# A fused two-block transformer kernel: output weights split beside the last z columns, output products tile by tile, head norms held back

## The reference

```
for layer in (0, 1):                               # first_block
    h = rms_norm(x) * (1 + scale) + shift          # shift, scale, gate = silu(c) @ ada_w + ada_b
    q, k.., v.., z = split(h @ w_in)               # 16 query heads, 4 key/value heads, 64 wide
    q, k = rope(rms_norm(q)), rope(rms_norm(k))    # the head norm
    o = attention(q, k, v)                         # layer 0: compressed + selected + window branch, gated
    x = x + gate * ((o * silu(z)) @ w_out)         # layer 1: one causal branch
# second_block ("layer 2"): the same skeleton with two kinds of heads, no z; two groups of 512 columns
# are normed before w_out; then PEER: h2 @ w_query, product keys, top 16, 16384 experts, final norm
```

## Time and profile before

| | |
|---|---|
| median of 3 runs | 1398.65 us (1395.99 to 1399.7) |
| the profiled execution | 1397.4 us, span 1396.0 us |
| PE busy | 1301.8 us (93%) |
| DVE busy | 1068.0 us (77%) |
| ACT busy | 592.2 us (42%) |
| POOL busy | 308.5 us (22%) |
| mean granted TensorE clock | 0.970 |

### The profile page before, as it was taken

One profiled execution on the slowest core, in us unless ns is written; L12 is line 12 of the kernel. 1 busy time (PEld: TensorE's weight loads), 2 busy tenths in 40 slices (PEclk: granted clock), 3 DMA queues, 4 the chain that ended last, 5 costly groups with the idle time before them and its releaser, 6 DMA issues.

```text
span 1396.0 us, 22037 instructions
## 1 busy us (share of the span) xinstructions
PE 1301.8 (93%) x8323; PEld 1125.2 (81%) x8323; DVE 1068.0 (77%) x2304; ACT 592.2 (42%) x1101; POOL 308.5 (22%) x199
## 2 busy tenths in 40 slices
PE   5898888988899789999999999999999999999997
PEld 5587754676498548999999999999988888888886
DVE  5586895688567868999958888888966666666666
ACT  0444681446232623455544444444443333333332
POOL 0364003371303032579990000000000000000000
PEclk9999899998999779999999999999999999999999
DMA  9867441666269416154444444444455555555552
GB/s 352 289 228 281 167 137 60 226 242 235 81 240 401 143 48 252 64 181 154 177 153 164 141 147 142 146 151 149 142 211 193 183 191 185 191 187 187 189 185 102
DMA packets 89935, 254.73 MB, mean 182 GB/s; under 512 B 8176, under 2 KB 15600, under 8 KB 89456
## 3 DMA queue, kind: packets, MB, share of 16 engines
q1 hardware_dynamic: 57424, 193.79, 39.9%
q10 hardware_dynamic: 32416, 59.66, 11.8%
HBM read 252.37 MB, written 1.05 MB: 182 GB/s over the span
## 4 chain that ended last, share of the span: by engine, by line
PE 66%; DVE 15%; POOL 7%; issue 4%; ACT 3%; DMA 3%; SPq 1%; ACTq 0%; POOLq 0%; DVEq 0%
PE bank L1692 25%; PE bank L1684 21%; PE bank L666 5%; PE bank L1963 4%; DVE arena L420 3%; PE bank L774 2%; POOL head_ms L797 2%; DVE u_lo L658 2%; POOL u_lo L1724 2%; PE bank L1090 2%; PE bank L992 1%; PE bank L901 1%; PE bank L692 1%; PE bank L545 1%; DVE arena L943 1%
## 5 line engine op out<-in xcount | busy, mean ns | idle before, releaser
L1684 PE MATMUL bank<-h_hi,u_hi 128*128 128x256 f32 x632 | 182.8, 289 | 4.0 <-POOL u_lo L1724 2.9
L1684 PE MATMUL bank<-h_hi,u_lo 128*128 128x256 f32 x632 | 178.7, 283 | 0.0
L1684 PE MATMUL bank<-h_lo,u_hi 128*128 128x256 f32 x632 | 178.7, 283 | 0.0
L2146 POOL TENSOR_SCALAR stat<-stat 128x1 f32<-128x1 f32 x2 | 0.4, 192 | 657.0 <-ACT arena L2143 657.0
L1684 PEld LDWEIGHTS bank<-h_hi,u_hi 128*128 128x128 f32 x632 | 121.0, 191 | 4.8 <-issue 1.8
L420 DVE CUSTOM_DVE_ANT_0 arena<-arena 128x1024 f32<-128x1024 f32 x80 | 117.3, 1480 | 7.0 <-DMA arena<-in_ada_t 6.0
L1684 PEld LDWEIGHTS bank<-h_lo,u_hi 128*128 128x128 f32 x632 | 121.1, 192 | 0.0
L1684 PEld LDWEIGHTS bank<-h_hi,u_lo 128*128 128x128 f32 x632 | 120.9, 191 | 0.0
L2059 ACT ACTIVATE u_hi<-raw 128x1024 fp32r<-128x1024 f32 x64 | 67.9, 1062 | 108.1 <-PE bank L1692 108.1
L1684 PE MATMUL bank<-h_hi,v_hi 128*128 128x256 f32 x392 | 112.9, 288 | 0.9 <-POOL v_lo L1724 0.9
L2059 ACT ACTIVATE v_hi<-raw 128x1024 fp32r<-128x1024 f32 x64 | 67.9, 1062 | 107.1 <-PE bank L1692 107.1
(11 more groups left out here) (275 smaller groups left out, 3552.2 us busy)
## 6 DMA issues: line engine op xcount, KB each, us to landing
raw<-in_u SPq DMA_DIRECT2D x128, 512.0 KB, 3.5
raw<-in_v SPq DMA_DIRECT2D x128, 512.0 KB, 4.3
arena<-in_ada_t SPq DMA_DIRECT2D x80, 512.0 KB, 4.6
arena<-in_ada_w SPq DMA_DIRECT2D x12, 512.0 KB, 12.1
raw<-in_nsa_w_in ACTq DMA_DIRECT2D x3, 2048.0 KB, 10.6
arena<-in_moba_w_in ACTq DMA_DIRECT2D x3, 2048.0 KB, 14.4
arena<-in_w_in ACTq DMA_DIRECT2D x3, 2048.0 KB, 10.0
arena<-in_w_query ACTq DMA_DIRECT2D x3, 2048.0 KB, 8.4
```

The lines of the kernel that those rows point to most:

```text
L1684: last = pe.matmul(zbank[k].t[:, 0:S], u[:, c, :], h[:, c, :], start=n == 0, stop=n == 3 * DC - 1)
```

## The change

Five things are changed. (1) The four parts of `second` are split beside the columns of `z1` (layer 2: beside `vb`), and its weights are therefore loaded beside `z0` (layer 2: beside `kb`), not at the start of attention. (2) In layers 0 and 1 the last column of `z1` is issued in step 0 of attention, in bank 7. (3) `rest` issues `second` of tile 0, then `first` of tile 1, then `second` of tile 1; tile 0's activations are split in step n-2 of attention, the subtraction on VectorE, in place of that step's `trickle(1)`. (4) `head_norm` is not issued behind `head_power` but held until the next tile's products and splits have been issued. (5) `trickle` units are shared out anew: 1 after a split tile (was 2), 3 after a z column (was 2), 6 after `qa` (was 4), 4+2+5 in `rest` (was 4+4+3); the last gate rows of layer 1 are no longer forced at the end of layer 0's `rest`. The fourth part of `kv1` is subtracted by GpSimd.

```diff
+    current, owed, row_free = [], [0], [False]
+    def next_row():
+        row_free[0] = False
+        m_row = load_silu(2, Y)
+        def next_silu():
+            make_silu(m_row)
+            fillers.remove("layer 0")
+        soon(next_silu, 6.0)
 def trickle(n):
                 if not fillers or isinstance(fillers[0], str):
+                    if "layer 0" in fillers[0:1] and row_free[0]:
+                        next_row()
...
+    held_seconds = []
+    def settle_held():
+        while held_seconds:
+            b, second = held_seconds.pop(0)
+            b.free = second()
     def settle_use(b, second, steps):
+        settle_held()
         trickle(steps)
-        b.free = second() if callable(second) else second
+        if callable(second):
+            held_seconds.append((b, second))
+        else:
+            b.free = second
... project
+                if ahead and c % 4 == 3:
+                    ahead.step()
+            settle_held()
             run_later()
-            if ahead:
-                ahead.step(2)
... project_split
                     if ahead:
                         ahead.step()
+                    if c == 3:
+                        settle_held()
-            settle_use(b, use(t, b.t[:], m), 2)
+            settle_use(b, use(t, b.t[:], m), 1)
... project_cols_split
-        for i in range(tile.n):
-            b = proj_bank()
+        def column(i, b):
             hi, lo, s = tile.parts[i]
...
             if ahead:
                 ahead.step()
+            settle_held()
             run_later()
             b.free = use(i, b.t[:, 0:S], m)
             trickle(steps)
             if i == 0:
                 load_all(loads)
+        for i in range(tile.n - (held_bank is not None)):
+            column(i, proj_bank())
+        if held_bank is not None:
+            return lambda: column(tile.n - 1, held_bank)
... attend
                 scores(p + 1)
+            if p == 0 and held:
+                held()
...
-            if p < n and (p or not causal_keys or len(branches) == 1):
+            if p == n - 2:
+                tile_halves()
+            elif p < n and (p or not causal_keys or len(branches) == 1):
                 trickle(1)
... gated_out
+        def second_tile(t, turns):       # the old loop's body: 24 products and add_rows(1, t, n, b, m)
         def rest(begin_next, turn_next, place_next, loads):
-            for t in range(NT):
-                split_h(t, G, oz_mark[t])
-            second.step(2)
+            split_h(1, G, oz_mark[1])
             trickle(4)
+            second_tile(0, None)
+            run_later()
+            begin_next()
+            trickle(2)
             first_chunks(1, range(DC))
-            second.step(2)
-            trickle(4)
+            load_all(loads)
             run_later()
-            for t in range(NT):
-                ...
-                if t == 0:
-                    begin_next()
-                    load_all(loads)
-                    trickle(3)
+            trickle(5)
+            second_tile(1, turns)
             if layer == 0:
-                ensure(1, (4, 5))
-                m_row = load_silu(2, Y)
-                ...
-                soon(next_silu, 8.0)
+                row_free[0] = True
-        return tail, rest
+        return tail, lambda: split_h(0, V, oz_mark[0]), rest
...
-    kv1 = Parts(columns(w_in, at_kv + WT), WT, False, [V] * 4)
+    kv1 = Parts(columns(w_in, at_kv + WT), WT, False, [V, V, V, G])
-        project_cols_split(z0, z_cols(zT, 0), z1, (out0,))
-        project_cols_split(z1, z_cols(zT, 1))
+        project_cols_split(z0, z_cols(zT, 0), z1, (out0, out1), 3)
+        last_column = project_cols_split(z1, z_cols(zT, 1), out1, held_bank=banks[7])
-        load_all((out1,))
...
-        project_cols_split(moba_z0, z_cols(zT, 0), moba_z1)
-        project_cols_split(moba_z1, z_cols(zT, 1))
+        project_cols_split(moba_z0, z_cols(zT, 0), moba_z1, (moba_out1,), 3)
+        last_column = project_cols_split(moba_z1, z_cols(zT, 1), moba_out1, steps=3, held_bank=banks[7])
-        load_all((moba_out1,))
...
-        project_cols_by_tile(qa, q_use(0), qb, (kb,), 4)
+        project_cols_by_tile(qa, q_use(0), qb, (kb,), 6)
-        project_cols_split(kb, kb_use, vb_tile)
+        project_cols_split(kb, kb_use, vb_tile, (mix_out1,))
-        project_split(vb_tile, v_use(vb))
+        project_split(vb_tile, v_use(vb), mix_out1)
-        load_all((mix_out1,))
```

More of the change, by code:

```diff
@@ L903, in add_outputs, with attend @@
         return inst
[L905 removed]
+    def attend(branches, q_of, bias_of, first_of, causal_keys, marks, v_marks, begin, done, tail, tile_halves, loads, sink=None, held=None):
         spare_pair[0] = 4
@@ L1101, in tail @@
             first_chunks(0, chunks)
+        def second_tile(t, turns):
+            x_hi, x_lo = (h[:, :, t * P:(t + 1) * P] for h in (h_hi, h_lo))
+            for n, cs in enumerate(halves):
+                b = proj_bank()
+                T.need(b.free, h_split[t])
+                for c in cs:
+                    if t == NT - 1 and c == DC - 3:
+                        turns()
+                    hi, lo, s = second.parts[c // 2]
+                    T.need(second.marks[c // 2])
+                    last = products(three(x_hi[:, c, :], x_lo[:, c, :], hi[:, c % 2, :], lo[:, c % 2, :]), b.t[:],
+                                    c == cs[0], c == cs[-1])
+                    if t == NT - 1 and c % 2 == 1:
+                        split_read[s] = m = T.did(last)
+                if t < NT - 1:
+                    m = T.did(last)
+                h_read[0] = m
+                add_rows(1, t, n, b, m)
+            pe_us[0] += 5.5
@@ L1481, in branch @@
                     lambda h, k: vs[i][:, k, (h // GQA) * HD:(h // GQA + 1) * HD], lambda h: h // GQA, gates[:, i + 1])
-        tail, rest = gated_out(out0, out1, 0, [b[1] for b in bufs])
+        tail, tile_halves, rest = gated_out(out0, out1, 0, [b[1] for b in bufs])
         attend([branch(0), branch(1)], lambda h, t: qT[half_of(h), h // 2, t * P:(t + 1) * P],
                causal_bias, lambda h: 3e38, True, [copied["q"], copied["k"], m_causal], [copied["v"]], cmp_values, times_z(zT),
-               tail, (moba_kv,))
+               tail, tile_halves, (moba_kv,), held=last_column)
         first_norm, factors, turn_first, place_first, finish = modulated(1, col("norm_g", 8, 16), 0, 8)
@@ L1626, in normed @@
             return oz_mark[t]
-        tail, rest = gated_out(mix_out0, mix_out1, 2, [carve([P, 512], s2) for _ in range(NT)], lambda t, half: rstds[:, t, half:half + 1])
+        tail, tile_halves, rest = gated_out(mix_out0, mix_out1, 2, [carve([P, 512], s2) for _ in range(NT)], lambda t, half: rstds[:, t, half:half + 1])
         attend([(lambda h, w: kaT[half_of(h), h // (HA // KVA), 0:w] if h < HA else kbT[half_of(h), (h - HA) // 2, 0:w],
@@ L1838, in build @@
         run_later(True)
+        assert not fillers, (fillers, current)
         A.need(split_read[3])
```

47 lines of the change are left out of this document (14 added, 33 removed).

## The result

The changed kernel is slower. Its median is 1424.54 us (1417.59 to 1426.75, 4 runs), against 1397.66 us for the kernel before (1395.99 to 1399.7, 4 runs); the ratio is 1.0181 with a 95% interval of 1.0149 to 1.0214. The prediction said 1385. A fifth run of the changed kernel, outside the median, took 1422.10 us. The profiled execution is the fastest of the four: 1417.59 us, span 1415.8, mean granted clock 0.960.

A forecast was written before the change was run, and what follows sets the result against it. Ahead of 575 us PE's idle time is what can be regained; later PE is busy throughout. Layers -10.6, -7.1 and +4.4 sum to -13.3: 1384.1 from 1397.4, forecast 1385 us as a median, range 1373 to 1396.

The forecast's parts named there:

- the output products: Stage behind each attention: new order removes PE's waits, gaining 7.9 us in layers 0 and 1 each, 9.7 in layer 2.
- the gate rows: Layer 0's end: the next layer's rows, no longer forced there, move into layer 1; gain 3.6 us, bounds 2 and 4.
- PE goes on without idle time: Sign: in layers 0 and 1 PE goes from the last `outputs` into L666 without idle time, stretch about 20 us.
- layer 2's late weights: Before layer 2's attention: ScalarE waits for `mix_out1`, landing no earlier than 454 us; cost 11 us, bounds 2 and 18.
- the tile halves: Tile 0's split in step n-2 delays the score read; cost 3.0, 3.8 and 2.8 us by layer, together 9.6.
- the z column: Last z column inside attention's step 0: cost 1.5 us in layer 0, 2.5 in layer 1; bounds 0 and 4 each.
- Held head norms: Projections: PE's waits for u_lo go; gain 3.6 us in layer 0 and 6.5 in layer 1.
- the bank is freed later, but four rotate: Remark on holding head norms: the later freeing of a bank was given no cost, since four banks rotate.
- The background units: Three units per z column: attention's start 1 us later in layer 1, not moved in layer 0.
- Two chunks more fall into the query stage, under DVE's slack: 0.3: Query stage: two extra background chunks on DVE fit under its slack, costing 0.3 us.
- Rival 3: ScalarE stands for output weights in layers 0 and 2, 10 us and 7 more, giving 1402 us; chance 0.06.
- Rival 4: Attention hides halves and column, but all attentions start 5 us later each: 1390 us; chance 0.22 shared with another rival.

The follow-up runs named there:

- e2: Changed kernel with layer 2's output-weight parts split behind attention's last group, not beside `vb`: layer 2's attention 59.6 to 49.9 us.
- e11: Kernel before plus tile 0's activation split in step n-2 and three more units behind `qa`, old output order: attentions 4.7, 3.5 and 1.6 us longer.
- e6: Changed kernel with the last z column of layers 0 and 1 issued before attention again: median 1421.4 us.
- e10: Kernel before with the held head norms alone: ratio 0.9996.
- e4: Changed kernel with each head norm issued directly behind its power again, not held: faster, layer 0's projection 123.8 us.
- e16: Kernel before with the new shares of background units alone: 9 us slower.
- e5: Changed kernel with the old shares of background units: attention 1 falls by 3.2 us, query stage to 62.7 us, layer 2's attention rises by 6.3.
- e14: Kernel before with held head norms and new unit shares together: 9.5 us above its theory of 1407; layer 0's projection 130.8 us.
- e1: Changed kernel with five instead of four background chunks issued in one go, the last before the searches: query stage 72.4 to 61.8 us.
- e3: Changed kernel with tile 0's activations split after attention again, by GpSimd, and step n-2's `trickle(1)` back: attentions 5.9, 3.8 and 3.0 us shorter.
- e7: Changed kernel with layers 0 and 1's output-weight parts split behind attention's last group, not beside z1: median as its theory had it (1415).

## Why the prediction was wrong

Right, by mechanism and size: the output products (with the gate rows -11.5, -7.9, -9.7 forecast; -12.4, -8.5, -11.4 in the profile; "PE goes on without idle time" holds); layer 2's late weights (11 forecast, 9.7 by e2); the tile halves (9.6 forecast, 9.8 in the attentions by e11); the z column at small cost (4.0 forecast, none told by e6).

Three of these agreements are in part luck. The halves were forecast at 3.0, 3.8 and 2.8 us and measured at 4.7, 3.5 and 1.6. Layer 2's weights were expected 3.3 us earlier in their stage than before; they landed as late as before (ScalarE goes on at 462.48, 67.5 us after the stage's start at 395.0; before, they landed at 457.3, and the stage started at 389.8). And layer 2's projection and attention, +13.8 forecast and +14.8 measured, hold 10.3 in attention, where all of the 13.8 was expected, and 4.5 in the projection, for which nothing was.

The failed steps:

1. **Held head norms, "Gain 3.6 and 6.5".** Alone they bring nothing (e10). Undone in the changed kernel, layer 0's projection is 6.8 us shorter (e4). I took a removed wait for removed time. The products that no longer waited for u_lo met the rope and the copies of the same norm one place later, and those I had dismissed with "the bank is freed later, but four rotate".
2. **The background units.** I priced the third unit per column at +1.0 for layer 1's start and at nothing in layer 0. Alone the shares cost 9 us, with 12.1 in layer 1's attention (e16): chunks are in DVE's order ahead of the score read, and in e16 they also wait 8.0 us for their own DMAs. In the changed kernel such a wait is 0.6 us (331.65), and undoing the shares gives 3.2 us of that attention back (e5).
3. **No step at all for their combination.** In layer 0 the moved gate rows and the held copy cost about 8 us together (e14 against e10 and e16), and the profile of the changed kernel has 5.7 of it as one wait. It is the kind of question that the prediction asked about weights and not about gate rows: what is queued ahead of the instruction that frees the bank.
4. **"Two chunks more fall into the query stage, under DVE's slack: 0.3".** DVE has slack there as a mean, but the consumer of the last chunk is PE's gate row, in order, and the searches lie ahead of the chunk: the stage is 9.7 us longer, and e1 takes 10.6 off it.

Against the sum: layer 0's projection and attention were forecast at +0.9 and came at +15.7, layer 1's at +0.8 and +10.4, layer 2's at +13.8 and +14.8, the query stage at +0.3 and +9.7.

Rival 3 named the right side with the wrong place: ScalarE had no wait for layer 0's output weights (its table of waits has no row for them), only the one on `z0` that was there before (6.65 us against 4.63). Rival 4's own sum was short: if halves and column both cost nothing, 13.6 comes off and not 9.6, which gives 1386 and not 1390.

The changed kernel's remaining 6.0 us at L1490, in layer 0's attention, are not attributed to one part: e3, e4, e6 and e7 keep 5.1 to 6.0 of it, e5, without the new units, has 2.6, and e14, with them and held norms but with the rest as before, 2.5; so the units move it most but do not make it alone, and no run isolates the rest. Nor is it settled why the changed kernel's four other runs lie 4.5 to 9.2 us above its profiled one.

## What to carry to other kernels

When background work is issued by count, its shares are part of the change: follow every chunk to the instruction that consumes it, and look at what stands ahead of it in its queue and whether its DMA has landed. A wait that a reorder removes is a gain only after the next operand, bank or copy in line has been shown to be earlier; try such a part alone. And when a bundle holds one sure gain, run it without its companions: here the early weights alone gave 0.9%, the new order of the output products with its two preconditions 1.1%, and the whole bundle lost 1.8%.

## What the runs showed of the hardware

**A small VectorE instruction can wait out the rest of a GpSimd one.** In the changed kernel a 128x8 scalar operation, which took 0.17 us the other time, took 1.68 beside a subtraction on POOL, and a 128x4 one, otherwise 0.16, took 2.25; both end with POOL's instruction (338.66 + 1.68 = 340.34 against 340.32; 317.15 + 2.25 = 319.40 against 319.38). The score reads, one of whose inputs is in PSUM, kept their 0.29 beside it:

```profile
338.45 0.29 DVE L982 CUSTOM_DVE_ANT_0 arena<-bank,causal 128x128 f32<-128x128 f32 x1
...
338.66 1.68 DVE L1007 TENSOR_SCALAR prob_scale<-rsum 128x8 f32<-128x8 f32 x1
...
317.15 2.25 DVE L427 TENSOR_TENSOR ada<-ada,cols 128x4 f32<-128x4 f32 x1
```
```profile
315.99 3.39 POOL L672 TENSOR_TENSOR v_lo<-arena,v_hi 128x1024 fp32r<-128x1024 f32 x1
...
337.98 2.34 POOL L672 TENSOR_TENSOR v_lo<-raw,v_hi 128x1024 fp32r<-128x1024 f32 x1 [14.07 <-ACT v_hi L669]
```

The Trainium skill (GPSIMD Engine Reference, Specifications) names this contention for VectorE instructions with two SBUF inputs or in a two-port mode. The 128x4 row agrees; the 128x8 row has one SBUF tensor input, so by that rule it would have to be the mode. No run here takes the two apart. In both rows the small instruction started after POOL's and ended with it.

**The held column costs two table loads.** Its Silu stands between exponentials, and ScalarE loads a table ahead of it and again behind it; e6, with the column before attention, has neither load. The prediction did not count them:

```profile
337.92 1.28 ACT L1194 ACT_TABLE_LOAD   x1
339.21 0.38 ACT L1194 ACTIVATE arena<-bank 128x256 f32<-128x256 f32 x1
339.61 1.28 ACT L990 ACT_TABLE_LOAD   x1
```

That is 2.6 us of ScalarE in step 0 of the attention, close to the 3.05 us of PE's wait that the column was to fill. It fits e6 finding no difference, but that the one eats up the other is argued and not shown.
